# Expert tiles of 32 slots on four TensorE column groups, in a two-layer mixture-of-experts backbone

## The reference

```python
# h (T, 1024): best of 4 groups, then the best 2 of its 4 experts, for each token
for e in range(16):
    y = (silu(h @ w_gate[e]) * (h @ w_up[e])) @ w_down[e]   # 1024x512, 1024x512, 512x1024
    out = out + gates[:, e:e + 1] * y                       # 0 where e was not chosen
```

## Time and profile before

| | |
|---|---|
| runs of the kernel | 967.37, 971.14 and 1878.71 us; median 971.14 |
| span of the profiled execution | 968.1 us (its own time lies between the two lower runs) |
| TensorE busy (PE) | 902.3 us, 93% |
| weight loads of TensorE (PEld) | 470.5 us, 49% |
| VectorE (DVE) | 387.6 us, 40% |
| ScalarE (ACT) | 258.0 us, 27% |
| GpSimd (POOL) | 115.9 us, 12% |
| DMA | 314.32 MB, mean 325 GB/s |
| layer 0's expert tiles | from 285.7 to 559.2 us |
| layer 1's expert tiles | from 740.9 to 958.7 us |

### The profile page before, as it was taken

The page is one execution under the profiler, slowest core; times in us unless marked ns, Lnnn a source line. Parts: engine busy times, 40 slices in busy tenths (PEclk is TensorE's granted clock), DMA queues, the critical chain, the costliest instruction groups (busy, mean ns, idle before and its releaser), DMA issues.

```text
span 968.1 us, 14234 instructions
## 1 busy us (share of the span) xinstructions
PE 902.3 (93%) x5142; PEld 470.5 (49%) x5143; DVE 387.6 (40%) x829; ACT 258.0 (27%) x418; POOL 115.9 (12%) x226
## 2 busy tenths in 40 slices
PE   3899999999979999999999969999988999999996
PEld 0444434343436656565656615447534544555453
DVE  2379999943662222222222234476353111111112
ACT  2413546432421111111112122046231111111112
POOL 2300000100021111111111130000002111011110
PEclk9999999999979999999999978999999999999999
DMA  9992397577488999989999994484467999999994
GB/s 350 349 380 92 139 379 264 180 269 291 172 335 343 423 425 424 421 321 419 382 427 423 394 338 154 178 312 184 174 226 267 422 418 424 424 421 428 423 425 167
DMA packets 68308, 314.32 MB, mean 325 GB/s; under 512 B 4668, under 2 KB 5088, under 8 KB 51888
## 3 DMA queue, kind: packets, MB, share of 16 engines
q1 hardware_dynamic: 54608, 275.78, 71.7%
q0 software_dynamic: 8992, 29.75, 8.3%
q10 hardware_dynamic: 4672, 8.30, 2.3%
HBM read 299.35 MB, written 14.47 MB: 324 GB/s over the span
## 4 chain that ended last, share of the span: by engine, by line
PE 83%; DVE 7%; DMA 4%; issue 2%; ACT 2%; SPq 2%; POOL 0%; ACTq 0%; DVEq 0%; POOLq 0%
PE ps L795 27%; PE ps L808 14%; PE ps L575 10%; PE ps L611 7%; PE ps L772 3%; PE ps L865 3%; PE ps L903 3%; PE ps L496 2%; DMA weight_ring<-in_ev_w_in 2%; PE ps L763 2%; SPq L362 2%; DVE arena L1096 2%; PE ps L804 2%; PE ps L943 1%; PE ps L595 1%
## 5 line engine op out<-in xcount | busy, mean ns | idle before, releaser
L795 PE MATMUL ps<-weight_ring,arena 128*64 128x256 f32 x1792 | 199.0, 380 | 5.0 <-issue 3.6
L795 PEld LDWEIGHTS ps<-weight_ring,arena 128*64 128x64 f32 x1792 | 140.2, 137 | 71.0 <-issue 20.2
L1393 DVE TENSOR_TENSOR arena<-arena,ps 128x128 f32<-128x128 f32 x78 | 19.0, 284 | 248.5 <-PE ps L795 248.5
L575 PE MATMUL ps<-hT,weight_ring 128*128 128x512 f32 x256 | 115.2, 605 | 2.0 <-DMA weight_ring<-in_ev_w_in 2.0
L808 PE MATMUL ps<-weight_ring,arena 128*64 128x512 f32 x448 | 102.3, 597 | 2.5 <-DVE arena L1406 0.2
L1096 DVE SCALAR_TENSOR_TENSOR arena<-arena,par 128x512 f32<-128x512 f32 x132 | 95.0, 750 | 5.5 <-PE ps L575 1.0
L1804 ACT ACT_TABLE_LOAD x39 | 50.0, 1283 | 129.8 <-issue 129.5
L575 PEld LDWEIGHTS ps<-hT,weight_ring 128*128 128x128 f32 x256 | 48.0, 192 | 66.3 <-issue 61.2
L795 PE MATMUL ps<-arena 128*64 128x256 f32 x704 | 78.0, 379 | 0.0
L611 PE MATMUL ps<-weight_ring,arena 128*128 128x512 f32 x160 | 70.8, 595 | 0.7 <-DVE arena L1543 0.5
L795 PEld LDWEIGHTS ps<-arena 128*64 128x64 f32 x704 | 56.2, 137 | 24.5 <-issue 5.9
(11 more groups left out here) (331 smaller groups left out, 915.3 us busy)
## 6 DMA issues: line engine op xcount, KB each, us to landing
weight_ring<-in_ada_w SPq DMA_DIRECT2D x24, 2048.0 KB, 14.9
weight_ring<-in_exp_w_gate SPq DMA_DIRECT2D x22, 2048.0 KB, 10.3
weight_ring<-in_exp_w_up SPq DMA_DIRECT2D x22, 2048.0 KB, 10.5
weight_ring<-in_exp_w_down SPq DMA_DIRECT2D x22, 2048.0 KB, 10.8
arena<-in_exp_w_gate SPq DMA_DIRECT2D x10, 2048.0 KB, 10.5
hT<-in_exp_w_down SPq DMA_DIRECT2D x10, 2048.0 KB, 10.8
arena<-in_exp_w_up SPq DMA_DIRECT2D x10, 2048.0 KB, 10.7
weight_ring<-in_ev_w_in SPq DMA_DIRECT2D x4, 2048.0 KB, 20.2
```

The source lines that it names most:

```text
L575: last = mm(ps[:, m % 4, :], wide(slot)[:, k, P * j:P * j + P], hT[:, k, :], start=(k == 0), stop=(k == KD - 1))
L795: last = mm(ps[64 * fh:64 * fh + 64, bank, 0:256], xgT[:, k % 4, 64 * (k // 4):64 * (k // 4) + 64], w[:, k, 256 * fh:256 * fh + 256], star ...
```

## The change

- Tiles of MT = 32 slots (40 tiles in layer 0, 24 in layer 1 for these inputs); a row is split into four quarters, 32 slots of each on 128 partitions. The tables are GMAX = 57 wide, with 15 thresholds.
- Gate and up of half the features are one product: `gate_up(hh)` streams 64 columns of each weight matrix (128 in all) on four column groups; the second call does the other half. Down runs on four column groups with 256 columns; the combine of layer 1 on four row groups.
- TensorE transposes nothing in a tile: VectorE's 32x32 block transpose makes `xgT` from `xg` and `actT` from `act_in`, in two halves.
- Gathers run four ahead (AHEAD), into four buffers with a semaphore each.
- The store of a tile's output moves from ScalarE's queue to GpSimd's, from four buffers. The lower experts' rows are gathered behind the last tile's store. GpSimd's tile loop is unrolled by four.
- A weight slot of gate or up is free when both halves are done (`end * 2 + 1`).
- The rows of the norm and of the modulation are contiguous now, without the dealt order; the end of layer 1 is one combine, then both squares, one root, and two scalings.

The diff, cut to its core:

```diff
-MT = 64
-GMAX = 34
+MT = 32
+MAXTILES = 48
+AHEAD = 4
+GMAX = MAXTILES + 2 * AHEAD + 1
...
                 if m < 2:
-                    sp.wait_ge(s_gu[l], end * 2 + m)
+                    sp.wait_ge(s_gu[l], end * 2 + 1)
...
-                        def gate_up(w, bank):
+                        def gate_up(hh):
                             for k in range(KD):
-                                for fh in range(2):
-                                    last = mm(ps[64 * fh:64 * fh + 64, bank, 0:256],
-                                              xgT[:, k % 4, 64 * (k // 4):64 * (k // 4) + 64],
-                                              w[:, k, 256 * fh:256 * fh + 256],
+                                for qd in range(4):
+                                    at = 256 * hh + 64 * qd
+                                    last = mm(ps[32 * qd:32 * qd + 32, 1 + hh, 0:P].rearrange("p (m n) -> p m n", m=2),
+                                              xgT[:, MT * k:MT * k + MT], w2[:, k, :, at:at + 64],
                                               start=(k == 0), stop=(k == KD - 1), skip_group_check=True)
                             last.then_inc(s_gu[l], 1)
-                        def act_transpose(c):
...
+                        def down(hh):
+                            pe.wait_ge(s_aT[l], g * 2 + (hh + 1))
+                            for c in range(2):
+                                step = 2 * hh + c
+                                for qd in range(4):
+                                    last = mm(ps[32 * qd:32 * qd + 32, down_bank, 0:256], actT[:, MT * step:MT * step + MT],
+                                              wd[:, step, 256 * qd:256 * qd + 256],
+                                              start=(step == 0), stop=(step == 3), skip_group_check=True)
                             return last
                         pe.wait_ge(s_xgT[l], g + 1)
                         weights(0)
                         weights(1)
-                        gate_up(wu, 2)
-                        tile_transposes(l, g + 2, 0, 2)
-                        act_transpose(0)
...
+                        gate_up(0)
+                        gate_up(1)
+                        pe.wait_ge(s_y[l], g + 1)
                         if l:
                             pe.wait_ge(s_spr, g + 1)
                             combine_tile()
                         weights(2)
+                        down(0)
+                        down(1).then_inc(s_dn[l], 1)
... on VectorE
+                def tile_columns(count):
+                    dve.wait_ge(s_xg[l], count)
+                    v.transpose(xgT.rearrange("p (k s) -> p k s", k=KD), xg.rearrange("p (i k) -> p k i", k=KD)).then_inc(s_xgT[l], 1)
                 with dve.Fori(0, total) as g:
+                    def act_columns(hh):
+                        half = slice(64 * hh, 64 * hh + 64)
+                        dve.wait_ge(s_sl[l], g * 2 + (hh + 1))
+                        v.tensor_tensor(act_in[:, half], act_sl[:, half], ps[:, 1 + hh, 64:P], ALU.mult).then_inc(s_ac[l], 1)
+                        dve.wait_ge(s_ac[l], g * 2 + (hh + 1))
+                        v.transpose(actT[:, half].rearrange("p (c s) -> p c s", c=2),
+                                    act_in[:, half].rearrange("p (i c) -> p c i", c=2)).then_inc(s_aT[l], 1)
+                    act_columns(0)
+                    if not l:
+                        v.tensor_copy(slot_cur[:, :], slot_tab[:, g, :]).then_inc(s_g2m, 1)
+                        dve.wait_ge(s_g2m, g * 2 + 1)
+                        v.scalar_tensor_tensor(g2_mat, g2_diff, slot_cur[:, 0:1], g2_lat, ALU.mult, ALU.add).then_inc(s_g2m, 1)
+                    act_columns(1)
+                    tile_columns(g + 2)
... on ScalarE
                 with act.Fori(0, total) as g:
+                    for hh in range(2):
+                        act.wait_ge(s_gu[l], g * 2 + (hh + 2))
+                        s.activation(act_sl[:, 64 * hh:64 * hh + 64], ps[:, 1 + hh, 0:64], ACT.Silu).then_inc(s_sl[l], 1)
-                        for hf in range(2):
-                            act.dma_start(rows[g, hf], y_sb[64 * hf:64 * hf + 64, :]).then_inc(s_yo, 16)
... on GpSimd
+                def four_tiles(j):
+                    for u in range(AHEAD):
+                        k, nxt = j * AHEAD + u, (u + 1) % AHEAD
+                        trips = 1 if nxt else 2
+                        pool.wait_ge(s_xgs[nxt], gathered(nxt, j + trips))
+                        pool.wait_ge(s_xgT[l], k + 1)
+                        bring(nxt)                                   # copy xg_in to xg
+                        g.tensor_copy(gcur[:, nxt:nxt + 1], gidx[:, bass.ds(k + (AHEAD + 1), 1)]).then_inc(s_gc[l], 1)
...
+                        gather(nxt, gcur[:, nxt:nxt + 1])
+                        if l:
...
+                        else:
+                            pool.wait_ge(s_y[0], k + 2)
+                            g.dma_start(places[k], y_sb[u]).then_inc(s_yo[u], 16)
+                            if not isinstance(j, int) or nxt == 0:
+                                pool.wait_ge(s_yo[nxt], (j + (trips - 1)) * 16)
+                                pool.sem_inc(s_yfree, 1)
```

More of the change, by code:

```diff
@@ L265, in build @@
         s_ac = [sem(f"expert_act{l}") for l in range(2)]
-        s_at = [sem(f"act_transposed{l}") for l in range(2)]
         s_aT = [sem(f"act_columns{l}") for l in range(2)]
@@ L269, in build @@
         s_y = [sem(f"tile_out{l}") for l in range(2)]
-        s_yo = sem("tile_out_stored")
+        s_yo = [sem(f"tile_out_stored{u}") for u in range(AHEAD)]
+        s_fill = sem("unused_rows_filled")
+        s_yfree = sem("tile_out_buffer_free")
         s_yg = [sem(f"expert_rows_in{t}") for t in range(NT)]
@@ L1252, in tmp, with large @@
                     return rt(l, at[0] - size, size)
+                def large(size):
+                    if not l:
+                        return tmp(size)
+                    spare[0] += size
+                    assert spare[0] <= D
+                    return mb[0][:, spare[0] - size:spare[0]]
                 def ranks(src, m):
@@ L1903, in _ @@
             act.wait_ge(s_cb, total + 1)
-            next_rms(1, 0)
-            act.wait_ge(s_cb, total + 2)
-            next_rms(1, 1)
+            for i in range(NT - CT):
+                if i:
+                    act.wait_ge(s_ss[4], i)
+                s.activation(quarters(junk), summed(i), ACT.Square, accum_out=ss[:, 1, i:i + 1]).then_inc(s_ss[4], 1)
+            rms(rstd[:, 1, 0:NT - CT], ss[:, 1, 0:NT - CT], D, 4, NT - CT)
         @block.gpsimd
@@ L1964, in _ @@
             pool.wait_ge(s_in, 9)
-            for i in range(2):
-                g.dma_start(y_dram[E * MT + TOK * i:E * MT + TOK * i + TOK, :].rearrange("(t p) d -> p t d", p=P),
-                            x[:, :, :]).then_inc(s_fill, 16)
+            for i in range(3):
+                rows = y_dram[E * MT + TOK * i:min(E * MT + TOK * i + TOK, (MAXTILES + AHEAD) * MT), :]
+                g.dma_start(rows.rearrange("(t p) d -> p t d", p=P), x[:, 0:rows.shape[0] // P, :]).then_inc(s_fill, 16)
             def row_in(dst, src, done):
@@ L1988, in _, with quarter_rows, moe @@
             row_in(mb[5], mod_dram[0][LAT, 1], s_nr)
-            def moe(l):
+            def quarter_rows(dst, src):
+                for qd in range(4):
+                    g.dma_start(dst[32 * qd:32 * qd + 32, :],
+                                src[256 * qd:256 * qd + 256].unsqueeze(0).to_broadcast([32, 256])).then_inc(s_g2, 16)
+            def moe(l, before=None):
                 tiles = toks(l)
@@ L2015, in moe @@
                     g.dma_start(mod_dram[1][3].rearrange("(k n) -> k n", n=P), mod_rows[3]).then_inc(s_mst, 16)
-                    pool.wait_ge(s_mst, 160)
+                pool.wait_ge(s_xgs[0], gathered(0, 1))
+                pool.sem_inc(s_pool, 1)
+                bring(0)
+                pool.wait_ge(s_xg[l], 1)
+                gather(0, gidx[:, AHEAD:AHEAD + 1])
+                if l:
+                    pool.wait_ge(s_mst, 128)
                     pool.wait_ge(s_rp[l], 2)
-                    for hf in range(2):
-                        g.dma_start(g2_mat[64 * hf:64 * hf + 64, :],
-                                    mod_dram[1][3, 512 * hf:512 * hf + 512].unsqueeze(0).to_broadcast([64, 512])).then_inc(s_g2, 16)
+                    quarter_rows(g2_mat, mod_dram[1][3])
@@ L2045, in moe @@
+                four_tiles(0)
+                with pool.Fori(1, (total + (AHEAD - 1)) >> 2) as j:
+                    four_tiles(j)
+                rounds = (total + (AHEAD - 1)) >> 2
+                if not l:
+                    expert_rows(total)
+                for u in range(AHEAD):
+                    pool.wait_ge(s_xgs[u], gathered(u, rounds + (1 if u else 2)))
+                    if not l:
+                        pool.wait_ge(s_yo[u], rounds * 16)
                 pool.sem_inc(s_pool, 1)
```

(10 more changed lines are left out.)

312 lines of the change are left out of this document (122 added, 190 removed).

## The result

| kernel | median of its runs | span profiled | granted clock |
|---|---|---|---|
| before | 971.56 us (967.37 to 974.92, and one run of 1878.71) | 968.1 us | 0.982 |
| after | 981.49 us (980.64 to 983.86) | 980.9 us | 0.924 |

The ratio is 1.0099, 95% interval 1.0074 to 1.0124. The forecast was 953, range 938 to 985: the time is inside, the forecast's sign is wrong. That it lies inside is the width of the range and not its reasons: the one case of the prediction that ends near 980 needs tiles of over 6 us in layer 0, and they take 5.44.

The account below looks back on a forecast made before the run. TensorE was taken to bound layer 0 and the weight stream layer 1, with layer 0's bound moving to the stream. On 968.1 us: -20 + 1 + 3 + 1.5 = -14.5, so 953.6; forecast 953, range 938 to 985.

Parts of the forecast that it names:

- the one case of the prediction that ends near 980: Layer 0 rival: handoffs hold TensorE; at 6.8 us a tile no gain there, time 980; chance 0.17, centred on 970.
- Fewer slots, TensorE per tile: Expert tiles: 1472 slots become 1280, 1024 become 768; 5.5 us a tile in layer 0, 7 in layer 1.
- The rival of issue and weight loads: Gate and up: weight loads don't overlap, 56 ns an instruction, 9.2 us a tile, some 1,105 us; chance 0.10.
- Layer 0's stream: Layer 0's weights become the bound at 16.6 us an expert; last product near 533, 26 us earlier.
- Their chain moves as it is, so 26 becomes 20: Layer 0's end: lower gathers behind the last store lose 6 us; landing and additions otherwise move unchanged, leaving 20.
- the sign: Listed mark of a wrong prediction: layer 0's end moves less than its last product by more than 8 us.
- The queue's 68.6 us of waits for products: Weight queue in layer 0 waits 68.6 us for gate and up products, so TensorE holds that layer.
- Routing and start of layer 0: Wider tile tables and more thresholds before layer 0's tiles: +1 us; gathers and copy hidden by the gate table.
- Start of layer 1: Four gathers instead of two before GpSimd's first copy, then copy and transpose: about 2 us in layer 1.
- The stream of layer 1 pays for the late start: Layer 1's first chunks leave sooner, paying for the late start; last chunk lands at the same 953 us, old scale.
- Expert 15's two tiles and the end: End of layer 1: two tiles for 44 tokens +3 us; whole combine and both squares before the first scaling +1.5.
- The clock: TensorE's granted clock falls in weight waits; 0 to 3.5 us for each layer's last expert, inside the range, no own case.

Follow-up runs that it names:

- a7: Changed kernel plus, at each layer 0 tile, a 64-row memory-to-memory copy nobody waits for before layer 1's end (40 copies, 5.2 MB): 992.2 us, ratio 1.0218.
- b4: Kernel before plus, at each of layer 0's 23 tiles, a 112-row memory-to-memory copy nobody waits for before the end (5.3 MB): 982.2 us, ratio 1.0100.
- a2: Changed kernel with the fourth modulation chunk issued ahead of the first attention chunk: 977.0 us, ratio 1.0048.
- a5: a4 with ScalarE's root table load and squares, between the layers, ahead of reading the fourth modulation product, VectorE's sum behind the additions: 962.6 us, ratio 0.9906.
- b5: Kernel before with 0.86 us more products, into a bank nobody reads, in each of layer 0's 23 tiles: 987.0 us, ratio 1.0157.
- a1: Changed kernel with VectorE's layer 1 wait for the gate rows moved behind the first tile's transpose: 977.9 us, ratio 1.0053.
- a3: Changed kernel with the edits of a1 and a2, and layer 1's first copy on GpSimd behind the second gather instead of the fourth: 972.0 us, ratio 0.9993.
- a4: a3 with VectorE's wait for layer 1's gate rows moved to just ahead of the scaling of a tile's output: 969.4 us, ratio 0.9964.
- b1: Kernel before with the fourth modulation chunk issued ahead of the first attention chunk: 970.1 us, ratio 0.9989.

## Why the prediction failed, step by step

- **Fewer slots, TensorE per tile: right.** Gate and up 3.68 us (3.5 forecast), combine 1.15 (1.5), tile 5.44 (5.5) and 6.43 (7), handoffs hidden but for some 0.2 us, by estimate (down takes 2.13 us in a tile of layer 0, and 1.93 in layer 1, where the combine covers the handoff). The rival of issue and weight loads is out: 128 instructions in 3.68 us are 29 ns each, not 56, in every tile at full clock. The Trainium skill (TensorE: Matmul & The Clock Gate, section Back-to-back issue gap) gives about 81 ns for a matmul of 128 columns with its weight load; on four column groups of 32 columns the trace disagrees, 58 ns for a matmul of the code, which is two instructions here, 29 ns each.
- **Layer 0's stream: 7 us off.** An expert takes 16.83 us (393.02 to 510.82, seven experts), not 16.6, and at expert 8 the stream was 2.9 us behind that of before instead of 2 ahead. The last chunk left at 522.76 instead of 515.4, so the last product came 17.8 us earlier than before and not 26.
- **"Their chain moves as it is, so 26 becomes 20": the failed step.** The chain that it names did move: the first gathered rows are added 11.6 us earlier, the 17.8 of the last product less the 6 that the step took off. But the start of layer 1 hangs on a second thing, which the step put at nothing: the fourth modulation chunk, which landed at 572.3 before and at 573.3 after. It stands in a queue of bytes: from 524 us on two expert chunks still under way, four modulation chunks, an attention chunk and 4.2 MB of gathered rows, 18.9 MB, by estimate 47 us at 402 GB/s. In both profiles the chunk lands at 572 to 573, though the last product differs by 17.8 us. Shown by a7 and b4 (bytes alone cost 11.6 and 9.7 us where their estimate is 13, in b4 through this very chunk), by a2 (another order of the same bytes gives 5 us) and by a5 (another order of the work around the chunk gives 5.6 more). I had quoted the DMA share of 1.01 as a property of the tiles and not asked what it was behind them: from 524 to 577 us it is 1.02 before and 1.04 after. The prediction had named the sign, an end of layer 0 that moves less than the last product by more than 8 us; it is 18.5.
- **One bound was read where there are two.** The queue's 68.6 us of waits for products were taken to mean TensorE. For the tiles that was right: b5's added products move the last one by all of their 20 us, b4's bytes by 2.9. For the start of layer 1 it was not: b5's 20 us of products cost 15 us of time, b4's 13 us of bytes 9.7. With both near their limit (TensorE busy for 96% of the stretch, the DMA engines for 98%), freeing one gave nothing.
- **Routing and start of layer 0: forecast 1, measured 2.7** (first products at 288.43 against 285.69), mostly hidden by the stream: its first chunk behind them leaves at 308.87 against 308.48.
- **Start of layer 1: forecast 2, measured 8.7** (10.0 at the first products, less the 1.3 brought along). The step counted two more gathers and looked at no wait. VectorE's wait for the gate rows stood at the same place before, where VectorE had nothing to do until 748; the change moved the tile's transpose to VectorE, and so behind it. Shown by a1, a3 and a4. Another 2.1 us are the routing, 1.3 of them its table product (2.48 us against 1.14): 0.3 because it is wider (it takes 1.43 in a1 to a5), the rest because the granted clock was low (0.56 over it, 1.00 before).
- **The stream of layer 1 pays for the late start: in part.** From expert 3's first chunk to the last it took 193.8 us against 197.5; 3.7 of 12.9 us came back.
- **Expert 15's two tiles and the end: nearly right.** Forecast +3 and +1.5, measured 2.8 and 0.8.
- **The clock: inside the range, as said.** TensorE waits for weights at each expert's start and the mean granted clock fell from 0.982 to 0.924; in layer 1's first products it cost 2.9 us.
- **Small packets: no change, nearly right.** A chunk of layer 1 takes 5.13 us (771.97 to 951.57, 35 chunks) against 5.21, one of layer 0 5.61 against 5.53.

The forecast's sum was 14.5 us less, the spans give 12.8 more, 27.3 apart: 19.7 up to the start of layer 1 (19 forecast, the 20 less 1 for layer 0's routing; 0.7 lost), 8.5 in layer 1 up to the last chunk (forecast 0, as its earlier chunks were to pay for the late start), less 0.9 for expert 15 and the end.

a5 still misses the forecast (962.6 against 953; its span 958.5 against 953.6). Most of it lies between the layers: its first transposes start at 570.7, where the sum says 582.9 less 19, 563.9, and they wait for the fourth modulation chunk even there (landed at 565.9). The rest is open. Layer 1's own load of bytes was not varied. Nor was it tried whether TensorE, kept busy in its waits, would give the clock's share back.

## What to carry to other kernels

Before costing a faster compute stage, add up the bytes between two points that both need transfers, and compare with the rate: if the share is 0.98 already, as here, the stage's end may move and the next one's start not, until the order of the transfers changes too. Look at what lands second-last as well: here the chunk that nobody waited for had landed only 0.3 us before TensorE came to it. When work moves to another engine, list every wait that stands ahead of its new place; a wait that cost nothing where the engine was idle becomes the critical one. And try the edits of order on the old kernel too: the two between the layers were worth 1.1% on the new kernel and nothing on the old, which is how the worth of the change with its waits put right (0.8%, a5 against b1) came to light.

## What was not expected of the hardware

A chunk of 2.1 MB that lands in 11 us among its own kind took 30.0 us when it shared the engines with eight gathers and three chunks ahead of it (issued at 524.83, 530.57 and 539.52, not yet landed at 543.2). Four column groups of 32 columns sustain an instruction every 29 ns with their weight loads, at full clock, for whole tiles; behind a wait, where the granted clock had fallen toward 1.2 GHz (0.54 over layer 1's first tile), the same products take 5.1 to 6.6 us instead of 3.68.
